# Last two single-expert rounds scattered by token, row loads placed ahead of them, and a new order of expert rounds

## The reference, cut to what matters

```python
def moe(hn, ...):                       # 64 experts, each token goes to 8 of them
    ...
    def expert_block(args):             # tokens of one expert
        xb = t_pad[tok]
        hid = jax.nn.silu(xb @ w_gate[e]) * (xb @ w_up[e])      # 1024 -> 256
        return (hid @ w_down[e]) * g[:, None]                   # 256 -> 1024
    ...
    routed = jax.ops.segment_sum(yb..., tok_buf...)             # sum of a token's 8 rows
    return routed + shared
h = h + moe(rmsnorm(h, g_ffn[l]), ...)
return rmsnorm(h, g_final)
```

## Time and profile before

| | us |
|---|---|
| median of 3 runs (1235.84 to 1243.15) | 1242.52 |
| the profiled execution, its own time | 1239.09 |
| its span, first to last instruction | 1237.3 |
| TensorE busy | 1100.3 |
| first expert load issued | 609.95 |
| first gate and up matmul of the rounds | 610.90 |
| last matmul of the rounds ends | 1177.12 |
| row loads of the end begin | 1182.41 |

### The profile page before, as it was taken

The page is one execution under the profiler, slowest core; times in us unless marked ns, Lnnn a source line. Parts: engine busy times, 40 slices in busy tenths (PEclk is TensorE's granted clock), DMA queues, the critical chain, the costliest instruction groups (busy, mean ns, idle before and its releaser), DMA issues.

```text
span 1237.3 us, 13235 instructions
## 1 busy us (share of the span) xinstructions
PE 1100.3 (89%) x5027; PEld 527.9 (43%) x5027; DVE 396.4 (32%) x927; ACT 220.9 (18%) x481; POOL 147.0 (12%) x194
## 2 busy tenths in 40 slices
PE   5999798887799969998899999987999898989945
PEld 3444586654444454443444333332333342333412
DVE  1784565353211031039522222221212111211237
ACT  3211422343202041031011111110111110101111
POOL 3000005020000000000212121211212121111100
PEclk9999898988899998999899999998999898989979
DMA  6125332310135310323299999999999999999487
GB/s 200 69 82 122 65 103 43 136 68 1 62 117 229 142 62 1 100 109 137 109 417 387 404 417 421 420 421 408 415 419 410 410 411 373 422 416 370 170 326 323
DMA packets 75806, 300.53 MB, mean 243 GB/s; under 512 B 20725, under 2 KB 24090, under 8 KB 50138
## 3 DMA queue, kind: packets, MB, share of 16 engines
q1 hardware_dynamic: 63066, 265.01, 55.0%
q0 software_dynamic: 12672, 34.62, 7.1%
HBM read 282.03 MB, written 27.53 MB: 250 GB/s over the span
## 4 chain that ended last, share of the span: by engine, by line
PE 76%; DMA 10%; DVE 6%; ACT 3%; issue 3%; SPq 1%; POOLq 0%; POOL 0%; DVEq 0%
PE ps L682 25%; PE ps L1064 22%; PE ps L1080 12%; PE ps L1046 3%; DMA ring<-in_w_down 3%; DMA dw<-in_w_down 3%; PE ps L806 2%; PE ps L819 2%; DMA ring<-expert_rows 2%; PE ps L958 1%; PE ps L1026 1%; PE ps L934 1%; PE ps L1088 1%; DMA z<-in_g_final 1%; PE ps L665 1%
## 5 line engine op out<-in xcount | busy, mean ns | idle before, releaser
L1064 PE MATMUL ps<-ring,z 128*32 128x512 f32 (+2 forms) x1056 | 271.1, 597 | 2.8 <-issue 1.4
L682 PE MATMUL ps<-dw,act_t 128*128 128x512 f32 x576 | 250.2, 596 | 4.0 <-issue 3.1
L682 PEld LDWEIGHTS ps<-dw,act_t 128*128 128x128 f32 x576 | 109.7, 191 | 141.1 <-issue 140.0
L1080 PE MATMUL ps<-ring,act_t 128*64 128x512 f32 (+2 forms) x528 | 145.7, 641 | 17.0 <-issue 14.0
L1064 PEld LDWEIGHTS ps<-ring,z 128*32 128x32 f32 (+2 forms) x1056 | 88.3, 134 | 115.6 <-issue 113.4
L1064 PE MATMUL ps<-z 128*32 128x512 f32 (+1 forms) x272 | 80.3, 604 | 6.0 <-issue 5.8
L1064 PE MATMUL ps<-dw,z 128*32 128x512 f32 (+2 forms) x272 | 77.7, 594 | 0.0
L1922 DVE COPY z<-ps 128x512 f32<-128x512 f32 x44 | 30.4, 692 | 138.4 <-PE ps L1080 138.4
L1080 PEld LDWEIGHTS ps<-ring,act_t 128*64 128x64 f32 (+2 forms) x528 | 43.9, 140 | 71.0 <-issue 67.1
L1405 ACT ACTIVATE tok<-ps 128x256 f32<-128x256 f32 x44 | 16.9, 384 | 309.0 <-PE ps L1064 309.0
L2070 POOL COPY ixb<-tabs 128x1 uint32<-128x1 uint32 x88 | 16.6, 188 | 412.1 <-DVE z L1922 394.0
(11 more groups left out here) (304 smaller groups left out, 1221.1 us busy)
## 6 DMA issues: line engine op xcount, KB each, us to landing
ring<-in_w_gate SPq DMA_DIRECT2D x44, 1024.0 KB, 16.1
ring<-in_w_up SPq DMA_DIRECT2D x44, 1024.0 KB, 29.4
ring<-in_w_down SPq DMA_DIRECT2D x44, 1024.0 KB, 28.5
ring<-expert_rows SPq DMA_DIRECT2D x8, 2048.0 KB, 21.8
dw<-in_w_gate SPq DMA_DIRECT2D x10, 1024.0 KB, 16.4
dw<-in_w_up SPq DMA_DIRECT2D x10, 1024.0 KB, 29.4
z<-in_w_gate SPq DMA_DIRECT2D x10, 1024.0 KB, 15.1
z<-in_w_up SPq DMA_DIRECT2D x10, 1024.0 KB, 28.4
```

The source lines that it names most:

```text
L682: ins = pe.matmul(ps[0:m, bank0 + j, 0:n], lhs(w, q * 4 + c4, c4, j), rhs(w, q * 4 + c4, c4, j), start=(q == 0 and c4 == 0), stop=(q == le ...
L1064: ins = pe.matmul(ps[rows, 2 + r % 2, :], xtt[r % 2][:, c, rows], ring_wgu(x % NBUF)[:, :, c, :], start=(c == 0), stop=(c == NC_D - 1))
L1080: ins = pe.matmul(ps[rows, 5 + n, :], htt[r % 2][:, c, rows], ring_wd(x % NBUF)[:, c, n * 512:(n + 1) * 512], start=(c == 0), stop=(c == 1))
```

## The change

1. `GROUPS` becomes "ffHHFFHHfHfFTHTHTTHFHHHTTHFFHHFF": f marks the four preloaded experts, which now stand at rounds 0, 1, 8 and 10 instead of 0 to 3; the last two rounds are F.
2. Buffers are no longer x % 6. `place_weights` gives the preloaded experts buffers 0, 2, 1, 3 and each other expert the buffer that comes free first. So only buffers 0, 2, 4 and 5 turn over in rounds 0 to 7.
3. `LATE = 2`: rounds 42 and 43 scatter by token number into arrays of their own, `late_rows` (2 x 512 x 1024), 2 MB each. These are filled with zeros by two DMAs that GpSimd issues after the mixer's gelu, and the places in `expert_rows` that the two rounds would have filled get zeros from two indirect DMAs at the start of the stage, between gathers 2 and 3. Gather 3 waits for them.
4. SP waits for 42 scatters only, and loads pieces 0 to 5, then (after the late scatters) the two late arrays, then pieces 6 and 7: ten pieces of 2 MB in eight buffers, each as its buffer is free.
5. DVE adds a late array to `h` in one operation of 128x2048. It adds TensorE's sums of tiles 0 to 2 after the eighth piece, then finishes tile 0; tile 1 after the ninth, tile 2 after the tenth, and tile 3 last. `g_final` is loaded behind piece 5 and awaited after the eighth piece.
6. TensorE and ACT do the sums directly behind one compare (an If with the sums in both arms). Early semaphores are merged: constants with the parameter rows, positions and lambda vectors with the parameters of b and c.

```diff
-GROUPS = "FFFF" + "HFTHHFTHHFTHFHFTHHFTHHFTHHFH"
+PRELOAD = (0, 2, 1, 3)
+GROUPS = "ffHHFFHHfHfFTHTHTTHFHHHTTHFFHHFF"
...
+            b = min(range(NBUF), key=lambda b: (-1, b) if held[b] is None else (LAST_ROUND[held[b]], held[b]))
+            BUF[x], BEFORE[x] = b, held[b]
...
+    PIECES = [("rows", n, n) for n in range(6)] + [("late", b, b) for b in range(LATE)] + [("rows", 6, 6), ("rows", 7, 7)]
+    buffer_free = {0: (42, 42), 5: (43, 42), 6: (44, 43), 8: (44, 44)}
...
         for b in range(2):
-            sp.wait_ge(y_out[b], 8 * NR)
-        sp.wait_ge(s_rows, 1)
...
+            sp.wait_ge(y_out[b], 8 * (NR - LATE))
+        for n, (kind, src, buf) in enumerate(PIECES):
+            if n in buffer_free:
+                sp.wait_ge(e_gu, buffer_free[n][0])
+                sp.wait_ge(e_y, buffer_free[n][1])
...
+        for n, piece in enumerate(PIECES):
+            sum_piece(n, *piece)
+            if n == 7:
+                for i in range(NT - 1):
+                    add_banks(i, n + 1)
+                dve.wait_ge(s_rt, 16 * 5)
+            if n >= 7:
+                finish(n - 7)
+        add_banks(NT - 1, len(PIECES))
         finish(NT - 1)
...
-        for r in range(2, 4):
-            round_gather(r)
+        round_gather(2)
+        for r in range(NR - LATE, NR):
+            zero_late_slots(r)
+        pool.wait_ge(s_late, WRITTEN_EARLY)
+        round_gather(3)
```

More of the change, by code:

```diff
@@ L100, with place_weights @@
 LAST_ROUND = [max(r for r, u in enumerate(UNITS) if x in u[1]) for x in range(NE)]
+BUF, NTH, BEFORE = [0] * NE, [1] * NE, [None] * NE
+def place_weights():
+    held = [None] * NBUF
+    for b, x in zip(PRELOAD, FIXED_AT):
+        BUF[x], held[b] = b, x
+    for x in range(NE):
+        if x not in FIXED_AT:
+            b = min(range(NBUF), key=lambda b: (-1, b) if held[b] is None else (LAST_ROUND[held[b]], held[b]))
+            BUF[x], BEFORE[x] = b, held[b]
+            if held[b] is not None:
+                NTH[x] = NTH[held[b]] + 1
+            held[b] = x
+place_weights()
+FIRST_LOADS = [x for x in range(NE) if BEFORE[x] is None and x not in FIXED_AT]
+NEXT_LOADS = [x for x in range(NE) if BEFORE[x] is not None]
 def expert_column(x):
@@ L415, in hybrid_layer @@
     s_rows = sem("all_rows_scattered")
-    s_yl = [sem(f"rows_loaded{i}") for i in range(6)]
+    s_late = sem("late_rows_written")
+    s_yl = [sem(f"rows_loaded{i}") for i in range(8)]
     s_red = sem("half_rows_summed")
@@ L486, in hybrid_layer, with slots_needed @@
     block = ctx.enter_context(nc.Block())
+    def slots_needed(eng):
+        return eng.value_load(ti[0:1, 0:1], min_val=0, max_val=S)
     def needs_passes(eng):
-        return eng.If(eng.value_load(ti[0:1, 0:1], min_val=0, max_val=S) > 0)
-    again = [(NE - 1 - j) // NBUF + 1 for j in range(4)]
+        return eng.If(slots_needed(eng) > 0)
+    again = [BUF.count(j) for j in range(4)]
     def scattered(e, j):
@@ L1142, in _, with combine @@
         round_down(NR - 1)
-        with needs_passes(pe):
+        def combine():
+            for n, (kind, src, buf) in enumerate(PIECES):
+                pe.wait_ge(s_yl[n % 8], 16 * (n // 8 + 1))
+                for k in range(TOPK // 2):
+                    i = src // 2 if kind == "rows" else k
+                    if kind == "rows":
+                        start, stop = src % 2 == 0 and k == 0 and i < NT - 1, src == 2 * NT - 1 and k == TOPK // 2 - 1
+                    else:
+                        start, stop = src == 0 and i == NT - 1, src == LATE - 1 and i < NT - 1
+                    ins = pe.matmul(ps[:, i, :], ident, half_rows[buf][:, k, 512:D], start=start, stop=stop)
+                ins.then_inc(s_prs, 1)
+        with pe.If(slots_needed(pe) < 1):
+            combine()
+        with pe.Else():
             with pe.Fori(0, PASSES) as p:
@@ L1149, in _ @@
                 one_pass(p)
-        for n in range(2 * NT):
-            pe.wait_ge(s_yl[n % 6], 16 * (n // 6 + 1))
-            for k in range(TOPK // 2):
-                ins = pe.matmul(ps[:, n // 2, :], ident, half_rows[n % 6][:, k, 512:D],
-                                start=(n % 2 == 0 and k == 0), stop=(n % 2 == 1 and k == TOPK // 2 - 1))
-            ins.then_inc(s_prs, 1)
+            combine()
     @block.scalar
```

183 lines of the change are left out of this document (112 added, 71 removed).

## The result

The changed kernel takes 1246.84 us in the median of 20 runs (1244.12 to 1251.7), the kernel before 1241.63 (20 runs, 1235.84 to 1243.24): the ratio is 1.0052, 95% interval 1.0042 to 1.0062. That is no change by the prediction's 1% bound, and by the interval 5 to 8 us slower. The profiled execution took 1246.98 us, its span is 1245.1, against 1239.1 and 1237.3 before: +7.8 us of span. Some 2.5 us of that are chance: the execution that was profiled before the change ran that much under its kernel's median, the one after at it.

A forecast was written before the change was run, and what follows sets the result against it. DMA was taken to bound the rounds and the final loads. Span 1237.3 - 2.0 (last piece, rounds' +2 included) + 6.6 (DVE's tail) = 1241.9; 1243.7 on the execution's time, plus half the runs' 3.4: 1246.0, range 1229 to 1257.

The forecast's parts named there:

- Early semaphores and fills: Before the expert rounds: waiting for merged semaphores and filling the late arrays with zeros beside the w_out load would cost 0.
- Zero scatters: Start of the rounds: two indirect DMAs, 0.86 MB, cost 2 us (0 to 2); gather 3 waiting for them, 0.
- New order: Expert rounds: the changed order moves waits for weights but not their sum, 0 us, bounds -15 to +10.
- The busiest engines: Expert rounds: DMA engines carrying an expert's first slots move a row every time, finish later and bound the rounds, not the mean rate.
- First row load: End of the rounds: needs round 41's scatter instead of round 43's, so starts at 1168.7, 13.7 us earlier than 1182.4.
- Ten pieces: Final loads: two more pieces cost 9.8 us and late scatters beside them 2.0; last piece at 1223.9 against 1225.9.
- Late scatter of round 43: Final loads: issued at 1181, landing 8.6 us later, so piece 6 is issued at 1190, 12 us ahead; nothing starves.
- DVE's order, L + 18.0: Last sums on DVE: with L the tenth piece's landing, the end comes at L + 18.0 against L + 11.4, +6.6 us.
- the end that keeps up: Rival at the kernel's end: two DVE finishes hide in gaps, only 1.5 us are added, 1241 us; chance 0.15.
- the faster order: Rival in the rounds: the order removes real waits, TensorE ends near 1162, not 1179, total 1229 us; chance 0.17.
- the dry DMA: Rival in rounds 2 to 9: four turning buffers free too late, DMA's queue empties, 15 us lost, 1261; chance 0.14.
- the late landing of round 41's scatter: Rival before the row loads: it lands behind weight loads, delaying it and them 5 us, total 1251; chance 0.12.

## Why the prediction was right

The class and the mechanism held: the last piece comes no sooner in spite of the earlier start, and the finishes behind it make the loss. That the time is so near (1246.0 for 1246.84) is in part luck. The sum on the span gave +4.6 us, where the two executions lie 7.8 apart and the interval says 5 to 8: the last piece was put 2.5 us too early and the tail behind it 0.7 too short. Against that, 1.7 us were added for the spread of the runs, and 1243.7 + 1.7 is 1245.4, not 1246.0. (Half way from 1251 to 1261 is 1256, not 1257; neither slip changes a class.) By its own steps:

- *Early semaphores and fills, 0*: the fills were issued at 261.14, the DMA share is 1.00 at 270 to 280 and back at 0.18 at 280 to 290, and w_out's first matmuls stand at 320.93 instead of 322.26. Through before 290, as worked out. The six traces without fills begin the expert stage at 609.95 to 612.56, the seven with them at 602.03 to 611.60.
- *Zero scatters, +2, and gather 3*: they were issued at 612.77 and 614.82, gather 3 at 628.67, as forecast. TensorE's round 2 ended at 637.1 and it turned gather 3's tokens at 638.0, 0.9 late. They moved 0.72 MB and not 0.86. The +2 was a little small: the lengths of the rounds above show some 3 us, and the 0 for gather 3's wait may be part of that.
- *New order, 0*: shown by the run of the order alone (1.0008). Its places were half right: 1.2 us before round 3 and 3.2 before round 7 for 5 each, 4.9 before a down in round 5 and 4.3 before round 20 where none was expected, 11.0 instead of 20 at rounds 28 to 31, and one of 2.7 before round 41 for three of 1. The sum was nearly right: the new order gained 0.9 us, and with the zeros the rounds are 1.7 to 3.4 us longer than before in the six traces, for +2 forecast. That the profiled one ended at 1179.4 for 1179 hides 3.4 us more of rounds behind a stage that began 1.2 sooner.
- *The busiest engines*: argued, not shown. The run with full slots rules out the mean rate (2.7 us for 6.7 MB, where 16 were due). Which engine carries which slot was not looked at.
- *First row load*: 1168.35 for 1168.7, where two misses cancel: round 41's scatter was issued at 1165.64 for 1165, and landed in 2.7 us for 3.7.
- *Ten pieces*: mis-sized. The tenth came at 1226.4 for 1223.9. The term for the late scatters was 2.0 and measured 2.6, with 0.72 MB and not 0.86. The other 2.3 us (55.5 against 43.4 + 9.8) are in the loads themselves, with nothing beside them: one piece lands 6.35 us after the last instead of 4.9, and the gap that holds g_final is 7.2 us where it was 6.7 before. What makes the one long gap stays open.
- *Late scatter of round 43*: taken as 8.6 us, measured 13.7. "12 us ahead" became 9.1 (the late arrays are issued at 1195.03, piece 5 is taken up at 1204.14), the conclusion that nothing starves held.
- *g_final and the compare, 0*: shown by the run that moves the wait (1.0003).
- *DVE's order, L + 18.0*: 18.7, by the run without the three finishes (-7.3 us) and by the reordered one (-4.6). The one thing in it that wasn't foreseen is TensorE's slow clock behind its stop of 3.74 us, 1.05 us: the three bank sums begin 5.1 us before the tenth piece and not 6.1.

The rivals: the end that keeps up fell with the runs on DVE's order; the faster order and the dry DMA fell with the order alone and with the DMA share of 1.00 and more in each 50 us from 650 to 1100; the late landing of round 41's scatter took 2.7 us, not 8.6.

## What to carry to other kernels

Before bytes are moved off a late dependence, count what else must wait for them: here 14 us of earlier start were paid with 14.6 us more from the first row load to the last piece (58.1 for 43.4) and with three finishes that now stood behind it. Data that one engine has just made and another sums can be placed by a matrix of ones and zeros from SBUF instead of going out and back. When three engines are each nearly full, price the addition in instructions as the trace counts them, and let the loads that everybody waits for be issued before the long ones. And compare a stage's length, not its end: a stage that begins at another time in another execution can hide a cost of 3 us or make one up.

## What the runs showed of the hardware

- The landing time of an indirect scatter of up to 128 rows of 4 KB (the last two moved 0.36 MB each) depends on what stands in the queues: 2.7 to 4.3 us with nothing ahead of it, 6.2 with a scatter of zeros and two loads under way, 8.6 in the rounds, 11.6 and 13.7 beside six loads of 2 MB. A load of 512 KB issued behind six such loads took 32.15 us.
- The chain of waits ran over the late scatter's landing, though the DMA queues were full until then. The share of the DMA windows (1.02 at 1205 to 1210) and the run with the scatters out of the way showed that.
- After 3.74 us without a matmul TensorE's granted clock was 0.50 at 1210 to 1215, its 1.2 GHz level. With the stop filled a piece took 3.70 us, as before the stop.
- 6.7 MB more of gathered rows cost 2.7 us in a stage whose DMA share reads 1.00 throughout: that share, a mean over the 16 DMA engines, didn't tell how much room was left.
